# One attention head in a row of the work order instead of two, for the tiles whose mixing hides behind expert gathers

## The reference, cut to what matters

```
logits = q_i @ k.T + c_i[:, None] - c_t[None, :]       # 8 heads x 64, causal
p = softmax(where(causal, logits, -inf));  att = p @ v
merged = concat(rms_norm(att), rms_norm(pool), rms_norm(ssm));  x = x + merged @ w_out
```

```
u_sel, v_sel = u_tab[experts], v_tab[experts]          # (tokens, 128, 1024) each
x = x + (gates * gelu(h . u_sel)) @ v_sel
```

## Time and profile before

| | us |
|---|---|
| median of 3 runs | 1616.92 (1611.43 to 1619.36) |
| the profiled execution | 1616.36 |
| its span in the profile | 1614.6 |

### The profile page before, as it was taken

The page is one execution under the profiler, slowest core; times in us unless marked ns, Lnnn a source line. Parts: engine busy times, 40 slices in busy tenths (PEclk is TensorE's granted clock), DMA queues, the critical chain, the costliest instruction groups (busy, mean ns, idle before and its releaser), DMA issues. The chain is left out here.

```text
span 1614.6 us, 19582 instructions
## 1 busy us (share of the span) xinstructions
PE 1089.5 (67%) x6936; PEld 570.1 (35%) x6936; DVE 1091.3 (68%) x2504; ACT 539.2 (33%) x1626; POOL 626.1 (39%) x577
## 2 busy tenths in 40 slices
PE   7968765587585375877487477677768555655664
PEld 6738431242253133442164143333245211111111
DVE  7625799855489968566479958556469974445445
ACT  2132344253243431254234442235134432222222
POOL 1002534434277253334334343334324344444441
PEclk9789987789798787888889787878879877677678
DMA  9006999979999899999999999999999999999997
GB/s 391 30 30 239 422 420 422 407 315 422 411 420 420 357 412 422 421 420 421 421 392 421 421 421 421 421 416 420 421 382 421 421 411 421 421 421 421 422 421 310
DMA packets 86211, 623.54 MB, mean 386 GB/s; under 512 B 9952, under 2 KB 9952, under 8 KB 11104
## 3 DMA queue, kind: packets, MB, share of 16 engines
q0 software_dynamic: 73728, 536.90, 80.4%
q1 hardware_dynamic: 12384, 85.37, 12.9%
HBM read 621.19 MB, written 1.05 MB: 385 GB/s over the span
## 5 line engine op out<-in xcount | busy, mean ns | idle before, releaser
L521 POOL DMA_INDIRECT slot<-experts,idx x512 | 589.3, 1151 | 935.8 <-PE psum L1463 719.8
L1128 DVE CUSTOM_DVE_ANT_0 slot<-slot,h 128x1024 f32<-128x1024 f32 x512 | 617.7, 1229 | 396.4 <-DMA slot<-experts,idx 392.0
L1463 PE MATMUL psum<-slot,diag 64*64 64x512 f32 x4080 | 598.4, 736 | 319.5 <-ACT diag L773 312.4
L1463 PEld LDWEIGHTS psum<-slot,diag 64*64 64x64 f32 x4080 | 175.1, 165 | 689.4 <-ACT diag L773 371.7
L757 ACT ACTIVATE ge<-ge 128x4 f32<-128x4 f32 x129 | 26.5, 205 | 486.3 <-DVE ge L1128 479.2
L1430 PE MATMUL psum<-hT,ring 128*128 128x128 f32 x1024 | 136.7, 298 | 24.1 <-DMA ring<-weights 18.7
L757 ACT ACT_TABLE_LOAD x54 | 69.3, 1283 | 219.9 <-DVE ge L1128 219.6
L1430 PEld LDWEIGHTS psum<-hT,ring 128*128 128x128 f32 x1024 | 132.9, 214 | 27.2 <-issue 20.2
L773 ACT ACTIVATE diag<-cst,ge 128x64 f32<-128x64 f32 x510 | 136.2, 336 | 6.5 <-PE psum L1463 2.4
L764 ACT ACTIVATE ge<-ge,gate 128x1 f32<-128x1 f32 x512 | 109.0, 283 | 4.2
L1407 PE MATMUL psum<-ring,work 128*128 128x512 f32 x96 | 50.5, 675 | 18.1 <-DVE work L1036 18.1
(11 more groups left out here) (235 smaller groups left out, 1112.2 us busy)
## 6 DMA issues: line engine op xcount, KB each, us to landing
ring<-weights SPq DMA_DIRECT2D x32, 1152.0 KB, 9.7
ring<-weights SPq DMA_DIRECT2D x28, 1024.0 KB, 9.1
slot<-weights SPq DMA_DIRECT2D x12, 1024.0 KB, 21.7
slot<-experts,idx POOLq DMA_INDIRECT x512, 18.7
sml<-small SPq DMA_DIRECT2D x2, 1160.0 KB, 9.8
xs<-x SPq DMA_DIRECT2D x2, 512.0 KB, 8.2
out<-xs SPq DMA_DIRECT2D x4, 256.0 KB, 4.2
cst<-consts SPq DMA_DIRECT2D x1, 564.5 KB, 5.0
```

The lines of the kernel that those rows point to most:

```text
L521: pool.indirect_dma_start(out=slot[:, place(E), :], out_offset=None, in_=src, in_offset=bass.IndirectOffsetOnAxis(ap=idx[:, n % 2, e:e + 1 ...
L1128: ins = dve.tensor_tensor_reduce(u, u, h2[:, n % 2, :], 1.0, 0.0, ALU.mult, ALU.add, d[:, i:i + 1])
L1463: ins = pe.matmul(acc[HALF * half:HALF * half + HALF, i, :], diag[rows, d % DIAGS, :], slot[rows, place(E), D + half * 512:D + half * 512 ...
```

## The change

Attention of steps 1, 2 and 3 gets nine rows instead of five: row `att i` holds head i alone, and the turn and product with V of head i-1. The pieces `pool`, `mixp` and `sq` stay with the first, second and last of them. The work of each head is the same. The lists are four rows longer: 38 rows during step 0, and 35 during steps 1 and 2, over the same 32 quads.

```diff
@@ MIX
-       ("att2", "max2", "nrm2"), ("att3", "max3", "nrm3"), ("att4", "sq"), ("merge",), ("out0",),
+       ("att2", "max2", "nrm2"), ("att3", "max3", "nrm3"), ("att4", "max4", "nrm4"), ("att5", "max5", "nrm5"),
+       ("att6", "max6", "nrm6"), ("att7", "max7", "nrm7"), ("att8", "sq"), ("merge",), ("out0",),
@@ MIX1
-        ("att3", "max3", "nrm3"), ("att4", "sq"), ("merge",),
+        ("att3", "max3", "nrm3"), ("att4", "max4", "nrm4"), ("att5", "max5", "nrm5"), ("att6", "max6", "nrm6"),
+        ("att7", "max7", "nrm7"), ("att8", "sq"), ("merge",),
@@ ACT, att(n, i)
-                for h in (2 * i - 2, 2 * i - 1):
-                    if h >= 0:
-                        evict(n, h)
-                for h in (2 * i, 2 * i + 1):
+                if i:
+                    evict(n, i - 1)
+                for h in (i,):
@@ DVE, biggest(n, i) and norm_pair(n, i)
-                for h in (2 * i, 2 * i + 1):
+                for h in (i,):
...
-                norm_prob(n, 2 * i)
-                norm_prob(n, 2 * i + 1)
+                norm_prob(n, i)
@@ PE, att(n, i)
-                before = [h for h in (2 * i - 2, 2 * i - 1) if h >= 0]
+                before = [i - 1] if i else []
...
-                for h in (2 * i, 2 * i + 1):
+                for h in (i,):
```

## The result

| | us |
|---|---|
| kernel before, median of 4 runs | 1617.12 (1611.43 to 1619.36) |
| changed kernel, median of 4 runs | 1657.01 (1651.64 to 1663.64) |
| ratio | 1.0254, 95% interval 1.0208 to 1.0300 |
| profiled execution of the changed kernel | 1651.64, span 1649.8 |

The forecast was 1651.0, in a range of 1630 to 1665, with 0.90 on slower. Of all runs one execution is left out, of the kernel before with pairs in quads 0 and 13: 1623.69 us at a mean granted clock of 0.685, where the others of that kernel have 0.74 to 0.83.

What follows compares the result with a forecast made beforehand. The prediction took DMA bytes at 421 GB/s plus time with dry queues as the bound; 10.9 + 11.1 + 5.4 + 7.2 = 34.6 us on the profiled 1616.4 gave 1651.0 us, range 1630 to 1665.

Steps and rivals of the forecast that it cites:

- One sign of being wrong: In the changed kernel's profile, PE's idle time put down to the ring of weight chunks would show the prediction wrong.
- Middle of step 0: Pairs in quads 0/10, 0/15 and 0/21 lose 9.8, 5.2 and 6.2 us, less today's 10.3: +10.9 us.
- D: The end of a quad's dot products on DVE, from which the issue of held-back gathers is counted.
- The rule: A quad loses 4.7 us less its margin, first gather's issue to the previous quad's last landing, if that is positive.
- End of step 0: Route pair in 0/26 puts DVE behind, and normA in quad 1/0 delays the gathers of 1/3: +11.1 us.
- the pair in 0/26 counts in full: `route0` and `route1` in quad 0/26 put DVE, with nothing in reserve, 5.4 us behind: +5.4 us.
- Rival 2: Late weight chunks in 0/26 and quad 21 of steps 1 and 2 hold PE and additions: +12, 1663 us; chance 0.10.
- `normA` in 1/0: Start of step 1: ACT weights quad 1/0 only after the norm, so the gathers of 1/3 go out 5.7 us later.
- End of step 1: Two routes in quad 1/31 and normA in 2/0 turn a margin of 10.4 into -0.7: +5.4 us.
- End of step 2: Two routes in the last quad, without normA, take 8.2 us of a margin of 3.7: +7.2 us.
- Pairs in 10 and 21 of steps 1 and 2: They wait for nothing DVE does in the same quad, so a margin of some 7 us remains: 0.
- Table loads: Twelve more attention rows cost ACT 31 us, covered while it waits for the maximum: taken as 0.

## Why the prediction was right, and where it was off

**The direction and the kind of cause.** Right. The bytes and the work of the engines are unchanged but for ACT's table loads, the time went into dips of the DMA rate at the quads with two rows, and placing the same rows by hand takes all of it back (1603.82). One sign of being wrong showed in part: PE's idle time put down to the ring is 24.6 us over the run against 18.7 before, and 5.38 of it stands in 0/26, where the forecast missed. Elsewhere it is no cause: the kernel with all pairs placed has 26.1 us of it.

**Middle of step 0: +10.9 forecast, +10.1 measured.** All three dips are there, and the one of 0/15 is half as deep as before (6.2 against 11.5). The issue times, D + 12.2, 9.3 and 10.3 forecast, were 11.8, 10.6 and 11.05. The run with the pair in 0/6 qualifies it: with `backA` out of the wait the dip behind 0/10 is 3.3 us less, as the mechanism has it, and the pair costs as much in its new place. The rule prices a wait, not what a second pair close by does to D.

**End of step 0: +11.1 forecast, +22.5 measured. This is the term that was mis-sized**, in its step "the pair in 0/26 counts in full: +5.4". It counted only DVE's extra work. The runs show some 18 us for the pair: 9 for the first softmax, which ACT issues after both rows, and 9 for the late chunk, DVE's second route and the second softmax together. Rival 2 had named the chunk in 0/26, with 4 to 5 us, and 5.38 is what PE waited; but it had the additions alone behind it, not ACT's softmax and DVE. Quad 21 of steps 1 and 2, which it named too, lost nothing: PE waits 2.2 and 2.1 us for the chunk there, and the changed kernel runs at 421 GB/s from 610 to 840 and from 990 to 1220. The other half of the term, `normA` in 1/0 with 5.7, was exact (11.0 against 5.3 us after D).

**End of step 1: +5.4 forecast, +7.2 measured. End of step 2: +7.2 forecast, +4.7 measured.** Both have the right cause, by the runs that move `normA` and the pair of quad 31; the sizes miss by 2 us each, in opposite directions. What the margin at D stands at when a step ends depends on how far DVE has got by then, which I read off the kernel before; that is my reading, and no run tests it.

**Pairs in 10 and 21 of steps 1 and 2: 0 forecast, 0 measured**, in the same two stretches.

**Table loads: 0 forecast.** The value is borne out by the kernel with all pairs placed: 31.6 us more of ACT, and the time of the kernel with pairs in 0 and 31, which has two heads in a row. The reason I gave was wrong. The loads are not done while ACT waits, they stand behind the wait. That they cost nothing since the row is short and the margin of a lone attention row is wide is argued, not shown. By the Trainium skill, page "ScalarE: Activation LUTs", section "What ACT_TABLE_LOAD costs", a switch has a drain of 1.38 us beside the load. The changed kernel's timeline shows the load of the gelu at 583.15, 0.02 us behind an ACTIVATE that ends at 583.13, and the next ACTIVATE at 584.45, 0.02 us behind the load: the 1283 ns agree, no drain stands beside it, and what is measured here decides.

**Not forecast.** The first route rows of steps 2 and 3 lose 2 us less than before, perhaps since they come in a quad with more of a margin; and this profiled execution started 7 us ahead of the other. The near hit of 1651.0 on the profiled 1651.64 owes something to that: the sum of 34.6 stands against 42.5 of measured losses, 8 us short, and against 39.9 between the medians.

## What to carry to other kernels

Where a list of work is dealt over a fixed number of slots by proportion, its length is a schedule: four more rows moved pairs and a norm into places where the release of a buffer was queued behind them. Before two pieces share a slot, ask what the second needs (a result of the first by another engine, a weight chunk that the first must set free) and what all engines have put off to the end of the slot; one wait there is passed on to every engine. When you cost it, count the margin (issue of the next transfer against the landing of the last), and the backlog of the busiest engine beside the wait; in this kernel hand placement was worth 0.7% over the kernel before, with one head in a row or two.

## What the runs showed of the hardware

**The start comes in two lengths.** Windows of the first stretch, the kernel before and then the changed kernel (60 to 70 us alone); both run the same instructions there.

```profile
50.00:60.00 10.00, 7.75 (x37) 6.25 (x38) 4.63 (x11) 0.00 (x0) 0.00 (x0) 0.77 0.01 2
60.00:70.00 10.00, 10.00 (x38) 8.20 (x38) 3.33 (x9) 1.83 (x8) 0.00 (x0) 0.50 0.00 0
```

```profile
60.00:70.00 10.00, 10.00 (x81) 9.11 (x81) 7.83 (x15) 3.16 (x14) 0.00 (x0) 1.00 0.01 2
```

In 60 to 70 us PE is always busy in both, at a granted clock of 0.50 (1.2 GHz) in one, 1.00 (2.4 GHz) in the other, and does 38 matmuls against 81. Ahead of it, from 50 to 60, PE was busy 7.75 of 10 us in the one and 8.30 in the other. That does not tell them apart: the kernel with the change in step 1 only was busy 8.30 there too, and had 0.50 after it. The gathers then start some 7 us apart. Over the profiled executions the first 150 us have either 145 to 155 GB/s at a mean clock of 0.83 to 0.87 (before, and seven of the eleven experiments), or 169 to 172 at 0.91 or 0.92 (the changed kernel and the other four). It goes with no edit that I can see: kernels made from either of the two are in both groups. The median of some runs can fall on either side, so differences of a few us between two kernels were read from windows after 150 us.

**An instruction of DVE beside six of GpSimd.** In the kernel before, one that works on 128x16 numbers took 6.62 us:

```profile
497.27 6.62 DVE L1097 SCALAR_TENSOR_TENSOR idx<-ex 128x16 uint32<-128x16 f32 x1
```

```profile
497.35 2.06 POOL L497 TENSOR_TENSOR work<-rot 128x512 f32<-128x512 f32 x2
...
501.38 2.47 POOL L497 TENSOR_TENSOR rot<-rot,work 128x512 f32<-128x512 f32 x2
```

It starts at 497.27 and ends at 503.89, and the six operations of GpSimd (three rows of two) run from 497.35 to 503.85. The other 31 runs of this line in that kernel take 0.17 us at the median. With the pair of 0/26 in 0/22, and again with all pairs placed, one of the 32 takes 5.89 us, and both times it ends 0.05 us after the last of the same six operations (in the latter 488.66 to 494.55, against 488.00 to 494.50). In the kernel before with pairs in 0 and 31 none falls beside them, and none takes over 0.18 us. So the coincidence repeats in three kernels; that the one holds up the other is still inferred from the times, since no run here takes GpSimd's operations away.
